# Product-key experts: gates added into coefficients in DRAM by indirect DMAs, in place of one-hot products

## The reference

```python
q  = (h @ w_query).reshape(B, S, 8, 2, 128)             # 8 heads
s1 = einsum('bshd,nd->bshn', q[..., 0, :], sub_keys1)   # 128 keys
s2 = einsum('bshd,nd->bshn', q[..., 1, :], sub_keys2)   # 128 keys
v1, i1 = top_k(s1, 16); v2, i2 = top_k(s2, 16)
cand  = v1[..., :, None] + v2[..., None, :]             # 256 sums
top_v, pos = top_k(cand, 16)                            # 16 experts a head
expert_idx = i1 * 128 + i2 at pos
gates = softmax(top_v)
act = gelu(einsum('bpd,bphkd->bphk', h, expert_down[expert_idx]))
out = einsum('bphk,bphkd->bpd', gates * act, expert_up[expert_idx])
x   = x + gt2 * out
```

## Time and profile before

| | |
|---|---|
| median of three runs | 1856.47 us (1855.97 to 1857.95) |
| the profiled execution's own time | 1856.82 us |
| its span, first to last instruction | 1855.5 us |
| TensorE busy | 1711.2 us, 92% |
| VectorE busy | 1146.0 us, 62% |
| ScalarE busy | 464.6 us, 25% |
| GpSimd busy | 390.3 us, 21% |
| mean granted TensorE clock | 0.964 of 2.4 GHz |
| moved by DMA | 270.90 MB, 146 GB/s |

### The profile page before, as it was taken

One profiled execution on the slowest core, in us unless ns is written; L12 is line 12 of the kernel. 1 busy time (PEld: TensorE's weight loads), 2 busy tenths in 40 slices (PEclk: granted clock), 3 DMA queues, 4 the chain that ended last, 5 costly groups with the idle time before them and its releaser, 6 DMA issues.

```text
span 1855.5 us, 25611 instructions
## 1 busy us (share of the span) xinstructions
PE 1711.2 (92%) x10111; PEld 1276.2 (69%) x10111; DVE 1146.0 (62%) x2309; ACT 464.6 (25%) x825; POOL 390.3 (21%) x241
## 2 busy tenths in 40 slices
PE   6998998999799967886997999899999999999998
PEld 2334554544355447645797999888888888888887
DVE  5774223241243354423998999777777777777786
ACT  1003223120122231101175766411111111111211
POOL 0000000000000110000078444333333333333332
PEclk9999999999899968897999999999999999999999
DMA  9974333233633200033242333444454455554543
GB/s 342 349 271 171 112 117 126 100 136 128 213 122 128 91 1 3 22 117 116 84 167 92 102 108 103 150 167 167 168 187 170 157 187 177 174 175 158 186 157 142
DMA packets 123979, 270.90 MB, mean 146 GB/s; under 512 B 10594, under 2 KB 46802, under 8 KB 123732
## 3 DMA queue, kind: packets, MB, share of 16 engines
q1 hardware_dynamic: 88080, 230.39, 36.0%
q10 hardware_dynamic: 35780, 38.87, 6.0%
HBM read 263.44 MB, written 5.79 MB: 145 GB/s over the span
## 4 chain that ended last, share of the span: by engine, by line
PE 77%; DVE 15%; issue 2%; ACT 2%; DMA 2%; POOL 1%; ACTq 0%; SPq 0%; DVEq 0%; POOLq 0%
PE bank L477 25%; PE bank L880 12%; PE bank L882 12%; PE bank L884 12%; DVE hot L1528 5%; PE bank L892 5%; PE bank L864 3%; DVE hot L1526 3%; DVE ada_acc L1003 3%; PE bank L742 1%; PE bank L460 1%; DMA ada_b<-in_b_ada_dram 1%; PE bank L751 1%; PE bank L752 1%; PE bank L494 0%
## 5 line engine op out<-in xcount | busy, mean ns | idle before, releaser
L477 PE MATMUL bank<-slot,hT 128*128 128x512 f32 (+2 forms) x1088 | 478.5, 596 | 6.1 <-DVE hT L990 2.0
L477 PEld LDWEIGHTS bank<-slot,hT 128*128 128x128 f32 x1088 | 207.2, 194 | 247.5 <-issue 242.6
L1995 POOL TENSOR_TENSOR up_low<-slot,up_high 128x512 fp32r<-128x512 f32 x128 | 229.9, 1796 | 428.6 <-DVE up_high L1443 428.6
L880 PE MATMUL bank<-hT_high,dT_high 128*128 128x256 f32 x1024 | 294.8, 288 | 6.8 <-POOL dT_low L1991 6.8
L882 PE MATMUL bank<-hT_low,dT_high 128*128 128x256 f32 x1024 | 289.2, 282 | 0.0
L884 PE MATMUL bank<-hT_high,dT_low 128*128 128x256 f32 x1024 | 288.3, 282 | 0.0
L880 PE MATMUL bank<-up_high,A_high 128*128 128x512 f32 x512 | 206.3, 403 | 3.6 <-DVE A_low L1446 3.6
L1904 ACT CAST dT_high<-bank 128x512 fp32r<-128x512 f32 x256 | 145.0, 599 | 228.8 <-PE bank L892 226.8
L882 PE MATMUL bank<-up_low,A_high 128*128 128x512 f32 x512 | 202.0, 395 | 0.0
L884 PE MATMUL bank<-up_high,A_low 128*128 128x512 f32 x512 | 201.4, 393 | 0.0
L880 PEld LDWEIGHTS bank<-hT_high,dT_high 128*128 128x128 f32 x1024 | 194.3, 190 | 9.6 <-issue 7.5
(11 more groups left out here) (407 smaller groups left out, 2194.1 us busy)
## 6 DMA issues: line engine op xcount, KB each, us to landing
slot<-in_expert_down_dram SPq DMA_DIRECT2D x128, 512.0 KB, 4.6
slot<-in_expert_up_dram SPq DMA_DIRECT2D x128, 512.0 KB, 4.0
slot<-in_w_in_dram SPq DMA_DIRECT2D x27, 2048.0 KB, 7.9
P<-in_w_ada_dram ACTq DMA_DIRECT2D x24, 1024.0 KB
slot<-in_w_out_dram SPq DMA_DIRECT2D x4, 2048.0 KB, 7.9
slot<-in_w_query_dram SPq DMA_DIRECT2D x4, 2048.0 KB, 8.1
slot<-in_w_branch_sb_dram SPq DMA_DIRECT2D x2, 2048.0 KB, 7.8
slot<-in_w_branch_ret_dram SPq DMA_DIRECT2D x2, 2048.0 KB, 8.4
```

Of the source, the lines that this page charges most:

```text
L477: m = pe.matmul(sums, lhsT=lhs[:, k, t * P:(t + 1) * P], rhs=w[:, k, :], start=(k == 0), stop=(k == w.shape[1] - 1))
L880: pe.matmul(o, lhsT=lhs_high.bitcast(F32R), rhs=rhs_high.bitcast(F32R), start=start, stop=False, skip_group_check=True)
L1995: g.tensor_tensor(up_low[p % 4][:, CW:].bitcast(F32R), up_tile[p % 4][:, CW:], up_hi[p % 2][:, CW:], ALU.subtract).then_inc(up_low_pool, 1)
```

## The change

- `C_dram`, 16384 experts x 256 tokens of float32 (16.8 MB) in DRAM, takes the place of `C`. SP sets it to zero with one DMA from a 2 KB row of zeros, right behind the load of the `o_rwkv` weights.
- VectorE computes `places`, the address of each pick in `C_dram`: (first key x 128 + second key) x 256 + token.
- GpSimd issues 256 indirect DMAs that add: one for each head, pick and half of the tokens, each with 128 single words. Before each head it waits until all 32 of the head before have landed, since two heads may add to one word.
- The one-hot matrices, their matmuls, the copies into `C`, `v_apply`, `selT` and the transposes for it go. So do the trips of gelus through DRAM.
- AHEAD is 100 and EARLY is 24: one hundred gelu tiles stay in SBUF (`G`), 28 are late. GpSimd makes `dT_low` for tiles 0 to 23 only, VectorE for all later ones. The exponential of the gates stands behind the gelu of tile 20.
- For each up place SP loads its coefficient tile (128 KB, `coeff`, four buffers), and VectorE multiplies at all 128 places, not at 108.
- The first four up tiles are loaded right behind the first four down tiles.

```diff
@@ carve @@
-    C = carve("C", N_KEYS, S)
-    EARLY, MIDDLE = 20, 28
-    AHEAD = EARLY + MIDDLE
+    EARLY, AHEAD = 24, 100
     LATE = N_KEYS - AHEAD
+    G = carve("G", AHEAD, S)
+    C_dram = nc.dram_tensor("c_dram", [N_KEYS * N_KEYS * S, 1], F32, kind="Internal").ap()
@@ pe_experts @@
-        for n in range(EARLY, AHEAD):
-            for i in range(groups_by[n - EARLY], groups_by[n - EARLY + 1]):
-                pe_made(i)
+        for n in range(AHEAD):
             if n + 2 < AHEAD:
                 pe_tile_turn(n + 2)
             pe_tile_down(n)
@@ v_first_block @@
+        v.memset(zeros, 0.0).then_inc(zeros_set, 1)
@@ v_picks @@
+        v_own.settle(v.scalar_tensor_tensor(rank[:, 0], sel_key[:, 0], float(N_KEYS), sel_key[:, 1], ALU.mult, ALU.add))
+        for t in range(TT):
+            heads = slice(t * PEER_H, (t + 1) * PEER_H)
+            v.tensor_scalar(places[:, heads, :], rank[:, 0, heads, :], float(S), tokens[:, t:t + 1], ALU.mult,
+                            ALU.add).then_inc(picks_ready, 1)
@@ v_weigh @@
+        if n < AHEAD:
+            A = G[:, n, :]
         else:
+            A = gl[fresh_at[p] % 2]
+            clear(v, ("down", n))
+        v.wait_ge(coeff_in[p % 4], 16 * (p // 4 + 1))
+        v_own.settle(v.tensor_tensor(A, A, c, ALU.mult))
+        v_own.settle(v_high(A_high[p % 2], A))
+        v_low(A_low[p % 2], A, A_high[p % 2]).then_inc(weighed, 1)
@@ v_experts @@
+        for n in range(EARLY, AHEAD):
+            v_tile_turn(n)
         v_split_up(0)
+        clear(v, ("down", AHEAD - 2))
+        clear(v, ("down", AHEAD - 1))
         v_weigh(0)
@@ g_experts @@
-        for n in range(AHEAD):
+        for n in range(EARLY):
...
+        g.wait_ge(picks_ready, 3)
+        g.wait_ge(zeroed, 16)
+        for h in range(PEER_H):
+            if h:
+                g.wait_ge(scattered[h - 1], 16 * TT * TOPK)
+            for k in range(TOPK):
+                for t in range(TT):
+                    x = t * PEER_H + h
+                    g.indirect_dma_start(C_dram, bass.IndirectOffsetOnAxis(ap=places[:, x, k:k + 1], axis=0),
+                                         gates[:, x, k:k + 1], None, compute_op=ALU.add).then_inc(scattered[h], 16)
@@ s_chunks @@
+            if name == ("o_rwkv",):
+                sp.wait_ge(zeros_set, 1)
+                sp.dma_start(C_dram.rearrange("(p a b) o -> p a (b o)", p=P, b=CW),
+                             zeros.unsqueeze(1).broadcast_to([P, N_KEYS * S // CW, CW])).then_inc(zeroed, 16)
@@ s_experts @@
+    def s_coeff(p):
+        if p > 3:
+            sp.wait_ge(weighed, p - 3)
+        n = ups[p]
+        sp.dma_start(coeff[p % 4], C_dram[n * P * S:(n + 1) * P * S].rearrange("(e n) o -> e (n o)", n=S)
+                     ).then_inc(coeff_in[p % 4], 16)
...
-        for n in range(AHEAD + 2):
+        for n in range(4):
             s_down(n)
         for p in range(4):
             s_up(p)
+        for n in range(4, AHEAD + 2):
+            s_down(n)
+        sp.wait_ge(scattered[PEER_H - 1], 16 * TT * TOPK)
+        for p in range(4):
+            s_coeff(p)
```

More of the change, by code:

```diff
@@ L164, in program @@
     gate_shifted, gate_exp, picks_ready = sem("gate_shifted"), sem("gate_exp"), sem("picks_ready")
-    hot_made, c_copied, middle_out, middle_in = sem("hot_made"), sem("c_copied"), [sem(f"middle{j}_out") for j in range(2)], [sem(f"middle{j}_in") for j in range(2)]
+    zeros_set, zeroed, scattered = sem("zeros_set"), sem("zeroed"), [sem(f"scattered{h}") for h in range(PEER_H)]
+    coeff_in = [sem(f"coeff{j}_in") for j in range(4)]
     scaled_ready = sem("scaled_ready")
@@ L219, in program @@
     gt = carve("gt", D)
+    zeros = carve("zeros", CW)
     persistent_top = cursor[0]
@@ L386, in program @@
     up_tile = [slot[1][:, j * D:(j + 1) * D] for j in range(4)]
-    cursor[0] = slot_at + 4 * KT * CW
-    hot = [carve(f"hot{j}", 2, 4, P) for j in range(4)]
     cursor[0] = lasting_top
@@ L402, in program @@
     gl = [carve(f"gl{j}", S) for j in range(2)]
-    sel_at = cursor[0]
     A_high, A_low = ([carve(f"{n}{j}", S) for j in range(2)] for n in ("A_high", "A_low"))
[L405 to L408, removed]
+    coeff = [carve(f"coeff{j}", S) for j in range(4)]
+    TH = TT * PEER_H
+    gates, places = carve("gates", TH, TOPK), carve("places", TH, TOPK, dt=I32)
+    gelu_at = cursor[0]
     cursor[0] = hT_at
@@ L448, in program @@
     eq = [x.rearrange("p a n -> p (a n)").rearrange("p (a k r) -> p a k r", a=TH, k=TOPK) for x in (qT, sc.rearrange("p a b n -> p a (b n)"))]
-    iota4 = iota.unsqueeze(1).broadcast_to([P, 4, P])
-    picks = [x.rearrange("p (t h) k -> p t (h k)", t=TT) for x in (sel_key[:, 0], sel_key[:, 1], gates)]
-    cursor[0] = coeff_at
+    cursor[0] = gelu_at
     X_back, gt_back, scaled = carve("X_back", TT, D), carve("gt_back", D), carve("scaled", TT, D)
@@ L916, in pe_tile_up @@
         m.then_inc(tile_done, 1)
[L918 to L924, removed]
     def pe_experts():
@@ L1506, in v_picks @@
         v.tensor_tensor(gates, gates, gate_norm.unsqueeze(2).broadcast_to([P, TH, TOPK]), ALU.mult).then_inc(picks_ready, 1)
[L1507 to L1536, removed]
     def v_split_up(p):
@@ L1886, in a_query @@
         a_load(iota, table("iota"), peer_in)
+        a_load(tokens, table("tokens"), peer_in)
         a_squares(peer_tmp, 4)
@@ L1921, in a_tile_gelu @@
         a.activation(to, b, ACT.Gelu_apprx_tanh).then_inc(emptied(("down", n)), 1)
-        if EARLY <= n < AHEAD:
-            clear(a, ("down", n))
-            a.dma_start(gelu_dram[(n - EARLY) * P:(n - EARLY + 1) * P, :], to).then_inc(middle_out[n % 2], 16)
     def a_experts():
@@ L1929, in a_experts @@
         a_tile_turn(1)
-        for n in range(EARLY):
-            a_tile_turn(n + 2)
+        for n in range(AHEAD):
+            if n + 2 < AHEAD:
+                a_tile_turn(n + 2)
+            if n == EARLY:
+                a.wait_ge(picks_ready, 3)
             a_tile_gelu(n)
@@ L1935, in a_experts @@
                 a.activation(gates, gates, ACT.Exp).then_inc(gate_exp, 1)
-        for n in range(EARLY, AHEAD):
-            for i in range(groups_by[n - EARLY], groups_by[n - EARLY + 1]):
-                turn, u = i // 4, i % 4
-                b = held(a, ("made", turn, u)).rearrange("p (n a) -> p n a", n=4)
-                toks = slice(turn * 16 + 4 * u, turn * 16 + 4 * u + 4)
-                a.copy(C[:, EARLY:, toks].rearrange("p a n -> p n a"), b[:, :, EARLY:]).then_inc(c_copied, 1)
-            if n + 2 < AHEAD:
-                a_tile_turn(n + 2)
-            a_tile_gelu(n)
-        for j in range(2):
-            a.wait_ge(middle_out[j], 8 * MIDDLE)
         for p in range(N_KEYS):
@@ L2025, in s_up @@
             sp.wait_ge(tile_done, p - 3)
-        else:
-            held(sp, ("made", S // 16 - 1, p))
         n = ups[p]
         sp.dma_start(up_tile[p % 4], I["expert_up_2"][0][n * P:(n + 1) * P, :]).then_inc(up_in[p % 4], 16)
-    def s_middle(p):
-        k, n = fresh_at[p], ups[p] - EARLY
-        if k > 1:
-            sp.wait_ge(weighed, fresh[k - 2] + 1)
-        for j in range(2):
-            sp.wait_ge(middle_out[j], 8 * MIDDLE)
-        sp.dma_start(gl[k % 2], gelu_dram[n * P:(n + 1) * P, :]).then_inc(middle_in[n % 2], 16)
+    def s_coeff(p):
[4 more added lines that the diff above has]
+                     ).then_inc(coeff_in[p % 4], 16)
     def s_experts():
@@ L2045, in s_experts @@
             s_up(p)
+        for n in range(4, AHEAD + 2):
[3 more added lines that the diff above has]
+            s_coeff(p)
         for n in range(AHEAD + 2, AHEAD + 4):
             s_down(n)
-        for p in range(4):
-            if EARLY <= ups[p] < AHEAD:
-                s_middle(p)
         for p in range(N_KEYS):
```

67 lines of the change are left out of this document (16 added, 51 removed).

## The result

The changed kernel takes **2036.33 us** (median of four runs, 2035.5 to 2037.09), against 1857.21 us (1855.97 to 1859.91) for the kernel before beside it: a ratio of **1.096** (95% interval 1.0946 to 1.0974). It is slower. The forecast was 1823 us, and the time lies 46 us above the top of the range.

The account below looks back on a forecast made before the run. TensorE bounds most of the kernel, VectorE the coefficient stage and new up stage. First up matmul 1311.4 plus 502 up stage plus 7.6 tail gives a span of 1821.0, a time of 1822, rounded up to 1823 us; range 1808 to 1990.

Parts of the forecast that it names:

- The scatter: GpSimd's queue after about 1025 us: 256 indirect DMAs at 1.0 us plus 16 us of waits, ending at 1297, hidden.
- rival 1: Scatter late on GpSimd's queue: (c - 1.04) x 256 us lost at c us per indirect DMA; slower; chance 0.38.
- The upper end of 1.7: Scatter price if nothing overlaps: 1.7 us per indirect DMA, from a 128-row store's issue to landing; scatter ends at 1476.
- the 0.48 for a hidden scatter: Chance of the main forecast: scatter hidden behind down tiles, up stage at VectorE's pace; own range 1808 to 1843 us.
- The rival's variant with VectorE: Scatter: GpSimd cannot write while VectorE runs, stretching 1.0 to 1.53 us per DMA; time 1948 us; chance 0.1 of the 0.38.
- Zeros: The 16.8 MB zero write on SP's queue takes 147 us, thinly hidden in 160 us before the next loads at 784.
- Gates: Before the scatter: exponential after gelu 20 ends about 1020.4, gates take 1.9 us more, ready at 1022.3.
- Down tiles to 99: Down tiles 20 to 99 run at TensorE's pace, 3.69 us each; gelu 99 starts at 1309.7.
- The waits for landing: In the scatter, eight waits for a head's DMAs to land, 2 us each, 16 us together.
- Up stage at VectorE's pace: Up tiles: 128 x 3.55 us plus 28 late down tiles x 1.7 us, 502 us (488 to 516).
- VectorE as the limit of the coefficient stage: Kernel before, 1014 to 1187 us: 28 down tiles need 103 of 173 us, so 70 us are lost to VectorE.
- The granted clock: Rival 4, up stage: clock falls in 0.8 us holes but comes back; chance 0.03 of more than 30 us.

Follow-up runs that it names:

- experiment 5: Changed kernel with half the picks: VectorE makes all of `up_low`, GpSimd none, 1801.84 us; then ScalarE also casts `up_high` and VectorE weighs first at non-late tiles, 1784.22 us.
- experiment 7: Kernel before, with more down tiles beside the one-hot products: MIDDLE from 28 to 40, 1843.7 us (ratio 0.9937), and to 34, 1846.51 us (0.9941).

## Why the prediction was wrong, point by point

**The step that failed** is the price in "The scatter": "I take the middle, 1.0". The runs show 1.84 us, 1.54 of work and 0.30 of issue, so the scatter ends at 1509.8 and not at 1297. The size of one term was off; the mechanism was the one of rival 1, at the place and with the limit of 1.04 us that it names. Its formula gives (1.84 - 1.04) x 256 = 205 us, so 2028, and 2036 was measured; the rest lies in the up stage. The upper end of 1.7 was no bound: the issue to landing of another engine's plain store says nothing of how long GpSimd works on a list of addresses, nor of an add. And the midpoint between two rows that were both of another kind had no ground, though each us of the price moves the time by 256. Once the upper end bounds nothing, the 0.48 for a hidden scatter has no ground either. That 1990 misses by only 46 us is no merit: the range ends at the 1.7 that was no bound.

- *The rival's variant with VectorE* (1.53) came near in size by luck and is refuted: the spacing is the same with VectorE idle.
- *The Trainium skill* (DMA: Bandwidth & Descriptors, Anatomy of one DMA, SWDGE path) has 2.0 us for such a DMA. Read as a serial price it gave an end at 1537, against 1509.8 measured, nearer than the row-based 1.0. But that is luck, for the parts that it names don't agree: it calls the generation of descriptors small and puts most of the time on the write's confirmation, while here the engine itself is held for 1.54 us, and the landing, 3.0 us after the issue, overlaps the next ones. The Trainium skill (Perfetto Trace Analysis, DMA Instruction — SWDGE (GPSIMD)) says that the end of such an instruction is the end of descriptor generation. The traces agree, for the instruction ends after 1.54 us and the last of a head lands later (2.97 us idle before the second head).
- *Zeros*: right in being hidden. The write went out at 624.94 and landed 50.8 us later, not 147; the next load stood at 785.19.
- *Gates*: VectorE's last piece ended at 1021.3 (1022.3 forecast); the scatter began at 1023.89 (1025).
- *Down tiles to 99*: right, 1308.59 against 1309.7.
- *The waits for landing*: right in size, 15.5 us for the seven between heads and 1.6 for the last (SP issues the first coefficient load at 1511.46), against 16 for eight. From there to the first up matmul it was 3.8 us, against 3.3.
- *Up stage at VectorE's pace*: right in its bound and nearly in its size, 512.9 us against 502, VectorE 466.0 of 503 busy. With the scatter hidden it is 1312.15 to 1823.06, 510.9 us. The place was right (3.55); the late tile was priced at 1.7 us and took 2.05, and 28 x 0.35 = 10 us. That GpSimd's subtraction is what makes the multiply 1.5 us long is shown by experiment 5. The Trainium skill (SBUF — State Buffer, SBUF: two separate sides) calls the port pair that both share an exclusive lock: a VectorE instruction with two inputs in SBUF and a GpSimd instruction that reads SBUF block each other. The traces agree: the multiply takes 1.52 us, until just after GpSimd's subtraction ends (1647.09), and 0.42 us without it.
- *VectorE as the limit of the coefficient stage* ("70 us are lost to it"): wrong, as experiment 7 shows, for 62 us of them were TensorE's own work. The sum doesn't use it.
- *The granted clock* fell to 0.51 in the hole (1.2 GHz), where TensorE did nothing for 205 us, and the first up matmuls came 0.43 us apart, not 0.23. From the ninth on it was 0.23 again, so the first up tile took 4.50 us and not 2.77. Where TensorE had only the short holes of the up stage it was 1.00, as forecast.

## What to carry to other kernels

A loop of small indirect DMAs is work of the engine that issues them: count them, multiply by a measured queue time (here 1.84 us with an add, 1.26 without), and compare that with the cover before anything else. From 16 to 128 words the number of words hardly matters, so fill each DMA; more than 128 in one was not tried. Where a price has no row of its kind, measure it in a small kernel, or say that it has no upper bound and spread the chances by that. And ask whether an engine's help is free: GpSimd's half of a subtraction lengthened VectorE's multiply by more than it saved.

## What the runs showed of the hardware that had not been expected

- An indirect DMA of single words with an add holds GpSimd about 1.25 us plus 2.3 ns a word, and the next follows after 0.30 us; with 128 words the add is 0.58 us of the 1.54.
- With the add each word seems to be a packet of its own: the queue of the changed kernel has 36864 packets for 256 DMAs, 144 each, which is 128 words and 16 more (80 with 64 words, 32 with 16). Without the add 128 words take 32. The rows of the two, with the add first:

```profile
q0 software_dynamic: 36864, 0.15, 4.8%
```

```profile
q0 software_dynamic: 8192, 0.15, 0.3%
```

- A zero write of 16.8 MB from one small tile in SBUF takes 50.8 us, some 330 GB/s.
- One execution had some 340 us in which TensorE took most matmuls 2.8 us apart, and the later profile of the same kernel has no such stretch. The cause is open.
